# A two-layer hybrid DiT kernel: x turned for the router in pieces, picks from two parts, and a reordered seam between the layers

## The chip, the cores and the metric

The kernel runs on one core of one Trainium2 chip. The metric is the time of one execution on the device in microseconds (us); lower is better.

## What is computed

512 latent tokens and 256 context tokens of width 1024 go through two layers, in float32. A layer is an attention part (gated linear attention, neighbourhood attention, sliding window attention) and a mixture of 16 experts, in which each expert picks its tokens. Cut to what matters here:

```python
def expert_choice_ffn(h, w_router, w_gate, w_up, w_down):
    bsz, n, _ = h.shape
    cap = CAPACITY_FACTOR * n // N_EXPERTS      # 64 of 512 latent tokens, 32 of 256 context tokens
    aff = jax.nn.softmax(jnp.einsum('bnd,de->bne', h, w_router).astype(jnp.float32), axis=-1)
    g, idx = lax.top_k(aff.transpose(0, 2, 1), cap)
    xs = h[bidx, idx]
    hid = silu(xs @ w_gate) * (xs @ w_up)       # per expert
    y = (hid @ w_down) * g
    return jnp.zeros_like(h).at[bidx, idx].add(y)

for l in range(DEPTH):                          # update_ctx only in the first layer
    x = x + gt_a * rms_norm(mix @ w_out[l], g_post_a)
    xc = xc + cgt_a * rms_norm(mix_c @ w_out[l], g_post_a)         # if update_ctx
    h = modulate(rms_norm(x, g_pre_f), sh_f, sc_f)
    x = x + gt_f * rms_norm(expert_choice_ffn(h, ...), g_post_f)
    hc = modulate(rms_norm(xc, g_pre_f), csh_f, csc_f)              # if update_ctx
    xc = xc + cgt_f * rms_norm(expert_choice_ffn(hc, ...), g_post_f)
```

## The kernel before, in words

Tokens stand in tiles of 128: four latent tiles (0 to 3) and, in the first layer, two context tiles (4 and 5), which come first in `tiles(l)`. Each engine runs a program of its own, written out by hand and held together by semaphores; no scheduler orders anything. A function of one name, `route` or `post_att` say, exists once for each engine that has a part in it. PSUM has eight banks of 512 columns: `bank(n)`.

**Output projection and norm.** `w_out` makes one output tile of 128x1024 after the other in banks 0 to 3, two banks each, from the ring of weights (`ring`). `post_att` follows it tile by tile: ScalarE takes the sum of squares (`square`, line 613), VectorE forms the gated output and adds it to x (lines 1241 and 1245), ScalarE squares the new x (`norm_square`) and scales it into `XN` (`norm_scale`, line 630). ScalarE works with a lag: at step i it squares output i, then new x of tile i-1, then scales tile i-2. The scaled tiles are also stored in DRAM by GpSimd and SyncE, x as `xkeep` and XN as `xn_lat` and `xn_ctx`, from which the experts gather their rows.

**Turning.** When all tiles are scaled, `turn_x` transposes them on TensorE, 128x128 at a time, feature block by feature block (`KC` = 8), into banks 0 to 3. VectorE (`h_out`, line 1020) moves the latent part to `hT` with scale and shift, ScalarE (`h_ctx`) the context part, and TensorE may turn block k only when block k-2 has been moved.

**Router.** `route` multiplies `hT` by the router's weights (line 1834), sums the parts into logits (line 1839), and VectorE forms the softmax over experts. The affinities `AFF` are turned (line 1845) so that a row holds one expert's affinities: 16 rows of latent tokens, 512 wide, and from row 32 on 16 rows of context tokens. The picks are eight rounds of three VectorE instructions over 48x512: the eight largest values (line 1350), their places (1351), and their replacement by -1 (1352). Indices and values are then spread over 128 columns (`IDXW`, `VALW`), turned once more on TensorE, and give `rows_l` and `rows_c`, the row numbers of the gathers (lines 1363 and 1367). In the first layer TensorE meanwhile makes modulation rows of the next layer (`mod_rows`, line 1504, and `mod_cols`, line 1512); its program has them ahead of the turning of the picks.

**Experts.** They come in pairs. For each pair GpSimd gathers latent rows (line 545) and, in the first layer, context rows (547); TensorE turns them (line 1867) and multiplies by gate, up and down weights (1930, 2012). Weights come in units through eight slots in turn, loaded by SyncE (`big`, `work` and `ring` parts; lines 430 to 447); a slot is loaded anew when TensorE has used it. In the first layer outputs are added into DRAM by scatter-adds on GpSimd (lines 561 and 563).

**The seam.** After the last pair of the first layer GpSimd copies the context's x back into `X_CTX` (line 585), waits for that and for the scatter-adds, and reads the sums (line 595) into XN. VectorE adds the last expert's context part that TensorE has just made (line 1263). For latent tiles `whole` on TensorE adds the read sum, by a product with the identity (line 2089), and the last expert's part (line 2094) in PSUM. `output_square`, `new_x`, `next_square` and `normal` norm this, form the next layer's x and its norm; `turn_next` turns x by a product with a diagonal matrix `NORM` (line 2102), which also scales it, and `h_next` moves it to `hT`. Then the next projection starts (line 1580).

## Time and profile before

| | us |
|---|---|
| median of 3 runs | 2111.82 |
| lowest, highest | 2109.3, 2114.98 |
| profiled execution | 2108.1 |
| its span, first to last instruction | 2106.3 |

Over the span TensorE is busy for 91%, its weight loads for 43%, VectorE for 26%, ScalarE for 22% and GpSimd for 7%; the mean granted TensorE clock is 0.971 of full speed. Such shares are averages over stages with different limits. The table of 40 slices shows this: TensorE stands at 9 tenths in more than half of them, the DMA engines at 9 from a third of the span to past its middle and again over the last fifth. The rows further down are therefore read by stretch.

### The profile page before, as it was taken

What the parts mean: (1) busy time and instruction counts of PE and PEld (TensorE: products, weight loads), DVE (VectorE), ACT (ScalarE), POOL (GpSimd) and SP (SyncE); (2) the same over time, 40 slices, a digit from 0 to 9 for tenths busy, and PEclk for the clock granted to TensorE, in tenths of its full rate; (3) what the DMA queues carried; (4) which work ended last, traced back from release to release, by engine and by line L of the source; (5) the groups of instructions that cost most, each with busy time, mean ns of one, the idle gap of its engine ahead of it and who ended that gap; (6) DMA issues with size and microseconds to landing.
All of it is one profiled execution on the core that took longest, in us unless ns stands there. A gap on an engine that the chain in (4) does not pass through costs nothing.

```text
span 2106.3 us, 25003 instructions
## 1 busy us (share of the span) xinstructions
PE 1916.1 (91%) x10556; PEld 895.5 (43%) x10556; DVE 546.3 (26%) x1173; ACT 464.6 (22%) x967; POOL 157.6 (7%) x225
## 2 busy tenths in 40 slices
PE   5998998999879999999999899889993999988886
PEld 2655555774433333333333455447741333332232
DVE  1020564662240000000000402456625011111113
ACT  4132123442311011111111403124422111111111
POOL 0000010100000111101011000011001000000000
PEclk9999999999979999999999999999996999999998
DMA  9212068002469999999999512130018999999996
GB/s 404 103 40 80 3 267 348 24 12 80 180 254 418 401 403 387 388 394 400 388 385 363 202 40 80 40 138 27 8 60 324 390 427 427 425 428 427 425 428 272
DMA packets 54280, 541.80 MB, mean 257 GB/s; under 512 B 6528, under 2 KB 8704, under 8 KB 23216
## 3 DMA queue, kind: packets, MB, share of 16 engines
q1 hardware_dynamic: 36704, 488.82, 56.5%
q0 software_dynamic: 17344, 51.72, 7.4%
q8 instruction: 65, 1.06, 0.2%
q14 instruction: 23, 0.19, 0.0%
q10 hardware_dynamic: 144, 0.01, 0.0%
HBM read 516.80 MB, written 23.72 MB: 257 GB/s over the span
## 4 chain that ended last, share of the span: by engine, by line
PE 75%; DMA 13%; DVE 6%; ACT 3%; issue 2%; SPq 0%; POOL 0%; DVEq 0%; POOLq 0%; ACTq 0%
PE ps L1930 15%; PE ps L1580 10%; PE ps L2012 8%; PE ps L1804 7%; PE ps L1558 5%; PE ps L1938 5%; DMA ring<-in_wstream 5%; DMA work<-in_wstream 3%; DMA big<-in_wstream 3%; PE ps L1752 3%; PE ps L2019 2%; PE ps L1884 2%; PE ps L1690 2%; PE ps L1504 2%; PE ps L1550 1%
## 5 line engine op out<-in xcount | busy, mean ns | idle before, releaser
L1930 PE MATMUL ps<-ring,work 128*64 128x512 f32 x1536 | 347.2, 605 | 16.1 <-DMA ring<-in_wstream 11.7
L1423 DVE TENSOR_TENSOR work<-glao,ps 128x512 f32<-128x512 f32 x31 | 21.3, 687 | 795.3 <-ACT glao L882 411.6
L1930 PEld LDWEIGHTS ps<-ring,work 128*64 128x64 f32 x1536 | 110.0, 139 | 246.7 <-issue 230.5
L1580 PE MATMUL ps<-hT,ring 128*128 128x512 f32 (+1 forms) x592 | 206.3, 507 | 3.3 <-issue 2.6
L2012 PE MATMUL ps<-big,work 128*64 128x512 f32 x704 | 164.6, 605 | 2.1 <-ACT work L842 2.1
L1580 PEld LDWEIGHTS ps<-hT,ring 128*128 128x128 f32 x592 | 112.1, 190 | 96.1 <-issue 86.4
L1804 PE MATMUL ps<-ring,hT 128*128 128x512 f32 x320 | 138.7, 592 | 0.0
L1938 PE MATMUL ps<-ring,work 128*32 128x512 f32 x1024 | 119.6, 597 | 0.0
L1558 PE MATMUL ps<-ring,hT 128*128 128x384 f32 (+3 forms) x384 | 110.9, 451 | 0.0
L710 ACT ACTIVATE work<-ps,work 128x512 f32<-128x512 f32 (+2 forms) x120 | 81.9, 684 | 77.2 <-DVE work L1163 44.7
L1930 PE MATMUL ps<-big,work 128*64 128x512 f32 x384 | 86.5, 595 | 13.5 <-DMA big<-in_wstream 13.5
L1804 PEld LDWEIGHTS ps<-ring,hT 128*128 128x128 f32 x320 | 60.6, 191 | 73.6 <-issue 73.6
L1159 DVE TENSOR_REDUCE work<-ps 128x2 f32<-128x1024 f32 (+2 forms) x60 | 73.3, 1221 | 61.2 <-PE ps L1701 58.4
L1558 PEld LDWEIGHTS ps<-ring,hT 128*128 128x128 f32 x384 | 70.7, 190 | 39.6 <-issue 15.3
L2012 PEld LDWEIGHTS ps<-big,work 128*64 128x64 f32 x704 | 46.1, 138 | 92.7 <-issue 88.9
L1504 PE MATMUL ps<-ring,silu_c 128*32 128x512 f32 x384 | 52.9, 678 | 26.5 <-DMA ring<-in_wstream 24.7
L1752 PE MATMUL ps<-work,big 128*64 128x128 f32 x960 | 65.7, 279 | 5.4 <-DVE hT L1202 5.4
L646 ACT ACTIVATE big<-ps 128x512 f32<-128x512 f32 (+1 forms) x41 | 20.8, 508 | 205.4 <-PE ps L1580 201.8
L891 ACT ACTIVATE glao<-ps 128x512 f32<-128x512 f32 x16 | 9.6, 597 | 239.6 <-PE ps L1930 239.6
L1938 PEld LDWEIGHTS ps<-ring,work 128*32 128x32 f32 x1024 | 28.5, 109 | 77.0 <-issue 77.0
L882 ACT ACTIVATE glao<-ps 128x512 f32<-128x512 f32 x15 | 9.0, 597 | 234.7 <-PE ps L1930 234.7
L1752 PEld LDWEIGHTS ps<-work,big 128*64 128x64 f32 x960 | 51.2, 137 | 18.9 <-DVE hT L1202 8.8
(311 smaller groups left out, 2219.2 us busy)
## 6 DMA issues: line engine op xcount, KB each, us to landing
ring<-in_wstream SPq DMA_DIRECT2D x150, 2048.0 KB, 13.0
big<-in_wstream SPq DMA_DIRECT2D x68, 2048.0 KB, 15.3
hT<-in_wstream SPq DMA_DIRECT2D x12, 1024.0 KB, 31.1
work<-in_wstream SPq DMA_DIRECT2D x12, 1024.0 KB, 33.8
x_kept<-big POOLq DMA_DIRECT2D x14, 512.0 KB, 8.5
big<-x_kept POOLq DMA_DIRECT2D x12, 512.0 KB, 6.0
xn_lat<-big POOLq DMA_DIRECT2D x8, 512.0 KB, 11.1
big<-in_x_all SPq DMA_DIRECT2D x6, 512.0 KB, 7.5
```

What stands on the lines that cost most here:

```text
L710: S.activation(PR[2 * (q % 2) + j][:, 0:nl + CTX], head_scores(q, nl)[:, j, :], ACT.Exp, bias=st["neg"][:, j:j + 1], scale=SCALE, accum_ou ...
L1159: link(V.reduce_max(st["max"], head_scores(p, nl), AX))
L1504: last = T.matmul(ob[32 * j:32 * j + 32, :], CS32[:, kc, :], u[:, kc, :], start=kc < 4, stop=kc >= 4)
L1558: last = T.matmul(bank(n % 4, k_), hTv[:, kc, t * P:(t + 1) * P], v[:, kc, 0:k_], start=kc == 0, stop=kc == KC - 1)
L1580: last = T.matmul(bank(n % 4, tn), uw[:, j * D + kc * P:j * D + kc * P + P], hTv[:, kc, t0:t0 + tn], start=kc == 0, stop=kc == KC - 1)
L1690: T.matmul(place[j], q[j], k[j][:, k0:k0 + nl], start=False, stop=True)
L1752: T.matmul(PV[HD * i:HD * i + HD, :], TM[:, keys[i][j], c:c + HD], PTP[q % 2][:, i, j * P:(j + 1) * P], start=j == 0, stop=j == n - 1)
L1804: return T.matmul(bank(2 * (i % 2) + j), hTv[:, kc, t * P:(t + 1) * P], u[:, kc, :], start=kc == 0, stop=kc == KC - 1)
L1884: last = T.matmul(ob, PT_L[half][:, t * P:(t + 1) * P], YL[half], start=True, stop=True)
L1930: last = T.matmul(bank(m)[64 * h:64 * h + 64, :], XST[:, kc, e, 0:CAP_L], gate_up[j][kk][:, m * D + h * 512:m * D + (h + 1) * 512], start= ...
L1938: last = T.matmul(bank(2)[32 * g:32 * g + 32, :], XST[:, kc, e, CAP_L:CW], gate_up[j][kk][:, g * 512:(g + 1) * 512], start=kc == 0, stop=k ...
L2012: last = T.matmul(bank(6 if ctx_too else 3)[64 * g:64 * g + 64, :], HT[:, kc, 0:CAP_L], down[j][kc % 4 // 2][:, kc % 2, h * 512:(h + 1) * ...
```

## The change

- **x is turned in pieces.** In the first layer, TensorE turns the two context tiles after output 2 of `w_out` (16 transposes into banks 4 to 7). `turn_lat` replaces `turn_x`: it turns latent tiles 0 to 2, block by block, before it waits for the norm of the last tile, and then the last tile alone. ScalarE and VectorE share the moves to `hT` (`ACT_K`, `DVE_K`); `h_out` and the "f" part of `h_ctx` are gone. ScalarE squares and scales each tile in its own step, without the lag.
- **Picks from two parts.** The 512 latent tokens stand in two parts of 256, in rows 0 to 15 and 32 to 47 of the turned affinities; the context in rows 64 to 79. Eight rounds go over 80x256, the last without replacement. 64 picks of each part result, one list in falling order, the other reversed; for each place the greater of the two values is kept (`LATER`), and with it its index, plus 256 for the second part. Values are turned ahead of indices.
- **The seam.** The sum of the second latent tile is added by VectorE instead of by an identity product (`SUMMED`). Half of the context's `h_next` moves from ScalarE to VectorE. The orders of `new_x`, `normal` and `next_square` differ, and `outputs` of the last expert precedes the context's first `next_square` on ScalarE.
- **Copies.** GpSimd issues the two copies of the context's x in pair 4 of the experts, not after the last pair.

The diff, cut to its core:

```diff
+        SUMMED = [NLT, NLT + 1, 1]
...
                         if i < PAIRS - 1:
                             scatter_add(2 * i + 1)
-                    for c in range(NCT):
-                        pool.dma_start(X_CTX[:, c, :], xkeep[LAT + c * P:LAT + (c + 1) * P, :]).then_inc(sem(f"x_rows{NLT + c}"), 16)
+                        if i == PAIRS // 2:
+                            for c in range(NCT):
+                                pool.dma_start(X_CTX[:, c, :], xkeep[LAT + c * P:LAT + (c + 1) * P, :]).then_inc(sem(f"x_rows{NLT + c}"), 16)
...
-                for i in range(len(ts) + 2):
...
+                for i, t in enumerate(ts):
+                    act.wait_ge(sem("wo"), i + 1 + l * PER["wo"])
+                    square(ps[:, (i % 2) * D:(i % 2) * D + D], SQUARES, ss[:, t:t + 1], "psq")
+                    if i == 2 and l < DEPTH - 1:
+                        for k in range(KC // 2):
+                            act.wait_ge(sem("xT"), k // 2 + 1 + before("xT", l, "f"))
+                            last = h_part(k, 1, hTv[:, k, LAT:TOK], bank(4 + k // 2, CTX, k % 2 * CTX))
+                        last.then_inc(sem("h_ctx"), 1)
+                    if i == n - 1:
+                        for k in ACT_K:
+                            act.wait_ge(sem("xT"), turned + k + 1)
+                            h_part(k, 0, hTv[:, k, 0:3 * P], bank(4 + k % 4, 3 * P)).then_inc(sem("h_ctx"), 1)
+                    norm_square(l, "f", i, t)
+                    norm_scale(l, "f", i, t)
+                for k in range(KC // 2):
+                    act.wait_ge(sem("xT"), turned + KC + 1 + 2 * (k // 2))
+                    last = h_part(k, 0, hTv[:, k, 3 * P:LAT], bank(k // 2, P, k % 2 * P))
+                last.then_inc(sem("h_ctx"), 1)
...
-                h_next(range(KC // 2), 0)
+                h_next(range(KC // 2, KC), 0).then_inc(sem("h_ctx"), 1)
                 next_square(l, 0)
-                h_next(range(KC // 2, KC), 0).then_inc(sem("h_ctx"), 1)
...
+                next_square(l, 3)
                 act.wait_ge(sem("xT"), 2 + before("xT", l + 1, "a"))
                 h_next(range(KC // 2, KC), 1).then_inc(sem("h_ctx"), 1)
-                next_square(l, 3)
                 act.wait_ge(sem("xT"), 4 + before("xT", l + 1, "a"))
...
                     output_square(l, NLT + 1)
...
+                    outputs(i, e)
                     next_square(l, NLT)
-                    outputs(i, e)
                     next_square(l, NLT + 1)
...
+                def h_lat(ks):
+                    for k in ks:
+                        dve.wait_ge(sem("xT"), turned + k + 1)
+                        h_part(k, 0, hTv[:, k, 0:3 * P], bank(4 + k % 4, 3 * P)).then_inc(sem("h_t"), 1)
...
-                for i, t in enumerate(tiles(l)):
+                for i, t in enumerate(ts):
+                    if i == n - 1:
+                        h_lat(DVE_K[0:1])
...
-                    if i:
-                        rms(l, "f", i - 1, tiles(l)[i - 1])
-                rms(l, "f", i, t)
+                    if i == 2 and l < DEPTH - 1:
+                        for k in range(KC // 2, KC):
+                            dve.wait_ge(sem("xT"), k // 2 + 1 + before("xT", l, "f"))
+                            last = h_part(k, 1, hTv[:, k, LAT:TOK], bank(4 + k // 2, CTX, k % 2 * CTX))
+                        last.then_inc(sem("h_t"), 1)
+                    if i == n - 1:
+                        h_lat(DVE_K[1:3])
+                    rms(l, "f", i, t)
+                h_lat(DVE_K[3:])
+                for k in range(KC // 2, KC):
+                    dve.wait_ge(sem("xT"), turned + KC + 2 + 2 * (k % 4 // 2))
+                    last = h_part(k, 0, hTv[:, k, 3 * P:LAT], bank(k // 2, P, k % 2 * P))
+                last.then_inc(sem("h_t"), 1)
...
-                for i in range(NCT, NT):
-                    new_x(i)
-                    if i > NCT:
-                        normal(i - 1)
+                dve.wait_ge(sem("x_rows1"), ACC_READ)
+                dve.wait_ge(sem("comb"), 3)
+                V.tensor_tensor(XN[:, 1, :], XN[:, 1, :], ps[:, D:2 * D], ALU.add).then_inc(sem("acc"), 1)
+                new_x(2)
+                new_x(3)
+                dve.wait_ge(sem("xT"), 1 + before("xT", l + 1, "a"))
+                h_next(range(KC // 2), 0)
+                new_x(4)
+                normal(2)
+                normal(3)
+                new_x(5)
+                normal(4)
+                normal(5)
                 dve.wait_ge(sem("xT"), 2 + before("xT", l + 1, "a"))
                 h_next(range(KC // 2), 1)
-                normal(NT - 1)
...
                 for r in range(CAP_L // 8):
...
-                    link(V.match_replace(dst, VALS[0:48, sl], src, -1.0))
...
+                    link(V.max(VALS[0:m, sl], src))
+                    found = V.max_index(idxu[0:m, sl], VALS[0:m, sl], src)
+                    link(V.match_replace(dst, VALS[0:m, sl], src, -1.0) if r + 1 < CAP_L // 8 else found)
+                wide = [(0, 2, slice(0, CAP_L)), (32, 2, slice(None, None, -1))] + ([(64, 4, slice(0, CAP_C))] if ctx_too else [])
+                for src, dst, done in ((VALS, VALW, "vals"), (idxu, IDXW, "picked")):
+                    for r0, n, order in wide:
+                        last = V.tensor_copy(v3(dst[r0:r0 + NE, :], n), src[r0:r0 + NE, order].unsqueeze(1).broadcast_to([NE, n, P // n]))
+                    last.then_inc(sem(done), 1)
+                idx_t, val_t = bank(5, m), bank(4, m)
                 dve.wait_ge(sem("pickedT"), 1 + l * PER["pickedT"])
...
+                link(V.tensor_copy(APART, val_t[:, 32:32 + NE]))
+                V.tensor_tensor(LATER, APART, val_t[:, 0:NE], ALU.is_gt)
+                V.tensor_tensor(VALT[:, 0:NE], APART, val_t[:, 0:NE], ALU.max)
+                dve.wait_ge(sem("pickedT"), 2 + l * PER["pickedT"])
+                link(V.tensor_copy(IDXT[:, 0:NE], idx_t[:, 0:NE]))
+                link(V.scalar_tensor_tensor(APART, idx_t[:, 32:32 + NE], float(2 * P), IDXT[:, 0:NE], ALU.add, ALU.subtract))
+                link(V.tensor_tensor(APART, APART, LATER, ALU.mult))
+                link(V.tensor_tensor(IDXT[:, 0:NE], IDXT[:, 0:NE], APART, ALU.add))
...
+                    last = V.tensor_copy(rows_l[r, :], IDXT[r, 0:NE].rearrange("p (a e) -> p e a", e=2)[:, half, :])
...
+                    if i == 2 and ctx_too:
...
+                        pe.wait_ge(sem("xn"), NCT + before("xn", l, "f"))
+                        for k in range(KC):
+                            for t in range(NCT):
+                                last = T.transpose(bank(4 + k // 2, P, (NCT * (k % 2) + t) * P), XN[:, NLT + t, k * P:(k + 1) * P], ident)
+                            if k % 2:
+                                last.then_inc(sem("xT"), 1)
...
+            def turn_lat(l):
...
+                pe.wait_ge(sem("xn"), n - 1 + before("xn", l, "f"))
...
+                for k in range(KC):
+                    if k >= 4:
+                        by, ks = ("h_ctx", ACT_K) if k - 4 in ACT_K else ("h_t", DVE_K)
+                        pe.wait_ge(sem(by), done + ks.index(k - 4) + 1 + before(by, l, "f"))
+                    for t in range(3):
+                        last = T.transpose(bank(4 + k % 4, P, t * P), XN[:, t, k * P:(k + 1) * P], ident)
+                    last.then_inc(sem("xT"), 1)
+                pe.wait_ge(sem("xn"), n + before("xn", l, "f"))
+                for b in (0, 2, 1, 3):
+                    for k in (2 * b, 2 * b + 1):
+                        last = T.transpose(bank(b, P, k % 2 * P), XN[:, 3, k * P:(k + 1) * P], ident)
+                    last.then_inc(sem("xT"), 1)
+                pe.wait_ge(sem("h_t"), done + 5 + before("h_t", l, "f"))
+                pe.wait_ge(sem("h_ctx"), done + 5 + before("h_ctx", l, "f"))
...
+                pe.wait_ge(sem("vals"), 1 + l * PER["vals"])
+                T.transpose(bank(4, m), VALW[0:m, :], ident[0:m, 0:m]).then_inc(sem("pickedT"), 1)
                 pe.wait_ge(sem("picked"), 1 + l * PER["picked"])
                 T.transpose(bank(5, m), IDXW[0:m, :], ident[0:m, 0:m]).then_inc(sem("pickedT"), 1)
-                pe.wait_ge(sem("vals"), 1 + l * PER["vals"])
-                T.transpose(bank(4, m), VALW[0:m, :], ident[0:m, 0:m]).then_inc(sem("pickedT"), 1)
...
-                    pe.wait_ge(sem(f"x_rows{t}"), ACC_READ)
+                    summed = t in SUMMED
...
                         pe.wait_ge(sem("acc"), NCT)
-                    elif t >= 2:
-                        pe.wait_ge(sem("y_used"), t - 1 + before("y_used", l, "f"))
...
-                        T.matmul(bank(2 * (t % 2) + h), ident, XN[:, t, h * 512:(h + 1) * 512], start=True, stop=False)
+                    elif t == 2:
+                        pe.wait_ge(sem("y_used"), 1 + before("y_used", l, "f"))
+                    elif t == 3:
+                        pe.wait_ge(sem("acc"), NCT + 1)
+                    if not summed:
+                        pe.wait_ge(sem(f"x_rows{t}"), ACC_READ)
...
+                            T.matmul(bank(2 * (t % 2) + h), ident, XN[:, t, h * 512:(h + 1) * 512], start=True, stop=False)
...
-                        last = T.matmul(bank(2 * (t % 2) + h), PT_L[0][r, t * P:(t + 1) * P], YL[1][r, :], start=False, stop=True)
+                        last = T.matmul(bank(2 * (t % 2) + h), PT_L[0][r, t * P:(t + 1) * P], YL[1][r, :], start=summed, stop=True)
```

The order on TensorE from the end of the first layer's output projection to the turning of the affinities, before (line 1804 is the projection, 1528 the transposes of x, 1834 the router, 1504 a modulation row, 1845 the affinities):

```order
397 L1804 MATMUL ps<-ring,hT 128x512 x80
398 L1528 MATMUL ps<-cst,big 128x128 x48
399 L1834 MATMUL ps<-hT,router 32x512 x8
400 L1834 MATMUL ps<-hT,router 32x256 x8
401 L1839 MATMUL ps<-cst,work 128x16 x6
402 L1504 MATMUL ps<-ring,silu_c 32x512 x8
403 L1845 MATMUL ps<-cst,work 48x128 x4
404 L1798 MATMUL ps<-work,ones 128x512 x4
```

And now, with 1867 the projection, 1896, 1916 and 1921 transposes of x, 1930 the router and 1942 the affinities:

```order
397 L1867 MATMUL ps<-ring,hT 128x512 x32
398 L1896 MATMUL ps<-cst,big 128x128 x16
399 L1867 MATMUL ps<-ring,hT 128x512 x48
400 L1916 MATMUL ps<-cst,big 128x128 x24
401 L1921 MATMUL ps<-cst,big 128x128 x8
402 L1930 MATMUL ps<-hT,router 32x512 x8
403 L1930 MATMUL ps<-hT,router 32x256 x8
404 L1935 MATMUL ps<-cst,work 128x16 x6
405 L1567 MATMUL ps<-ring,silu_c 32x512 x8
406 L1942 MATMUL ps<-cst,work 80x128 x2
```

The 48 transposes that stood in one block behind the projection stand in three places: 16 inside it, 24 and 8 behind it; four transposes of affinities are two.

VectorE's order from the end of the last round of picks in the first layer to the row numbers, before:

```order
435 L1351 MAX_INDEX idxu<-work 48x8
436 L1352 MATCH_REPLACE work<-work 48x512
437 L1354 CAST work<-idxu 16x128
438 L1355 CAST work<-idxu 16x128
439 L1357 COPY work<-work 16x128
440 L1358 COPY work<-work 16x128
441 L1363 CAST rows_l<-ps 64x8 x2
442 L1367 CAST rows_c<-ps 32x8 x2
```

And now; the lines from 1417 to 1424 are the merge of the two parts:

```order
440 L1407 MAX_INDEX idxu<-work 80x8
441 L1413 COPY work<-work 16x128 x3
442 L1413 CAST work<-idxu 16x128 x3
443 L1417 COPY work<-ps 128x16
444 L1418 TENSOR_TENSOR work<-work,ps 128x16
445 L1419 TENSOR_TENSOR work<-work,ps 128x16
446 L1421 COPY work<-ps 128x16
447 L1422 SCALAR_TENSOR_TENSOR work<-ps,work 128x16
448 L1423 TENSOR_TENSOR work<-work 128x16
449 L1424 TENSOR_TENSOR work<-work 128x16
450 L1427 CAST rows_l<-work 64x8 x2
451 L1431 CAST rows_c<-ps 32x8 x2
```

The last round has no replacement. Between the turned picks and `rows_l` stand seven more instructions of 128x16, and the copies of the values precede the casts of the indices.

GpSimd's order in the last pairs of the first layer's experts, before (561 and 563 are scatter-adds, 545 and 547 gathers, 585 the copies of the context's x, 595 the reads of the sums):

```order
89 L561 DMA acc_lat<-work,add_l 1024x512
90 L563 DMA acc_ctx<-work,add_c 1024x256
91 L561 DMA acc_lat<-work,add_l 1024x512
92 L563 DMA acc_ctx<-work,add_c 1024x256
93 L585 DMA hT<-x_kept 128x1024 x2
94 L595 DMA big<-acc_ctx 128x1024 x2
95 L595 DMA big<-acc_lat 128x1024 x4
```

And now, from the middle pair on, where 566 and 568 are scatter-adds, 550 and 552 gathers and 591 the copies:

```order
77 L550 DMA big<-xn_lat,rows_l 128x1024
78 L552 DMA big<-xn_ctx,rows_c 64x1024
79 L566 DMA acc_lat<-work,add_l 1024x512
80 L568 DMA acc_ctx<-work,add_c 1024x256
81 L591 DMA hT<-x_kept 128x1024 x2
82 L566 DMA acc_lat<-work,add_l 1024x512
83 L568 DMA acc_ctx<-work,add_c 1024x256
84 L550 DMA big<-xn_lat,rows_l 128x1024
85 L552 DMA big<-xn_ctx,rows_c 64x1024
```

Five pairs of scatter-adds follow the copies, and the reads of the sums then follow the last of these (not shown).

## Rows read from the trace of the kernel before

**Rows 1.** Busy time by stretch: us, PE, PEld, DVE, ACT, POOL, clock, DMA share, GB/s.

```profile
640.00:700.00 60.00, 60.00 (x432) 20.84 (x424) 4.18 (x11) 8.36 (x18) 8.27 (x6) 1.00 1.02 404
...
1625.00:1634.00 9.00, 6.87 (x21) 2.76 (x22) 0.00 (x0) 4.18 (x9) 0.97 (x1) 0.50 0.20 58
1650.00:1660.00 10.00, 10.00 (x46) 3.28 (x44) 0.00 (x0) 1.18 (x2) 0.00 (x0) 0.92 1.01 431
```

**Rows 2.** TensorE in order of time, first layer: start, us, engine, line, what.

```profile
574.13 2.79 PE L1834 MATMUL ps<-hT,router 128*32 128x512 f32 x32 [0.75 <-DVE hT L1020]
...
579.34 3.31 PE L1504 MATMUL ps<-ring,silu_c 128*32 128x512 f32 x16
582.58 0.88 PE L1845 MATMUL ps<-cst,work 128*48 128x128 f32 x4
...
597.50 1.05 PE L1512 MATMUL ps<-cst,glao 128*128 128x2 f32 x8 [0.72 <-ACT glao L697]
...
609.94 1.94 PE L1867 MATMUL ps<-cst,big 128*128 128x128 f32 x8 [7.10 <-issue]
```

**Rows 3.** ScalarE at the end of the output projection, first layer, then second.

```profile
557.69 1.02 ACT L613 ACTIVATE work<-ps 128x1024 f32<-128x1024 f32 x1 [10.07 <-PE ps L1804]
...
563.13 2.17 ACT L630 ACTIVATE big<-big,small 128x1024 f32<-128x1024 f32 x2
...
1578.74 1.02 ACT L613 ACTIVATE work<-ps 128x1024 f32<-128x1024 f32 x1 [10.07 <-PE ps L1804]
```

**Rows 4.** TensorE between the layers, in order of time.

```profile
1146.70 0.66 PE L1906 MATMUL ps<-cst,work 128*128 128x128 f32 x4
...
1155.27 1.15 PE L1894 MATMUL ps<-work 32*128 32x256 f32 x16 [0.16 <-ACT work L855]
...
1194.27 10.56 PE L1580 MATMUL ps<-hT,ring 128*128 128x512 f32 x32 [2.07 <-issue]
```

**Rows 5.** VectorE, first layer: last new x, first and after last pick, row numbers.

```profile
560.59 1.22 DVE L1245 TENSOR_TENSOR big<-big,work 128x1024 f32<-128x1024 f32 x1
...
584.21 0.69 DVE L1350 MAX8 work<-work 48x8 f32<-48x512 f32 x1
...
601.51 0.22 DVE L1354 CAST work<-idxu 16x128 f32<-16x128 uint32 x1
...
602.81 0.33 DVE L1367 CAST rows_c<-ps 32x8 uint32<-32x8 f32 x2
```

**Rows 6.** TensorE, second layer: router, first expert.

```profile
1594.33 1.93 PE L1834 MATMUL ps<-hT,router 128*32 128x512 f32 x16 [0.91 <-DVE hT L1020]
...
1628.62 16.83 PE L1930 MATMUL ps<-ring,work 128*64 128x512 f32 x64 [2.13 <-ACT work L834]
```

**Rows 7.** GpSimd's queue between the layers.

```profile
1132.87 1.80 POOL L585 DMA_DIRECT2D hT<-x_kept  x2
1154.56 1.05 POOL L595 DMA_DIRECT2D big<-acc_ctx  x2 [19.89 <-DMA hT<-x_kept]
```

**Rows 8.** Landing times of L563, the scatter-add of context rows.

```profile
DMA to landing us min/median/max: 15.0/15.7/16.3
```

**Rows 9.** VectorE between the layers: the context rows' sums.

```profile
1159.37 2.35 DVE L1263 TENSOR_TENSOR big<-big,ps 128x1024 f32<-128x1024 f32 x2 [7.07 <-DMA big<-acc_ctx]
```

**Rows 10.** ScalarE between the layers: half of the context's turned tiles.

```profile
1174.80 1.93 ACT L757 ACTIVATE hT<-ps,cols 128x256 f32<-128x256 f32 x4 [2.41 <-PE ps L2102]
```

**Rows 11.** GpSimd's queue, second layer: the first gather.

```profile
1620.10 1.01 POOL L545 DMA_INDIRECT big<-xn_lat,rows_l  x1 [17.88 <-DVE rows_l L1363]
```

**Rows 12.** SyncE's queue, second layer: weight loads.

```profile
1598.44 0.99 SPq L430 DMA_DIRECT2D big<-in_wstream  x2
...
1601.63 0.45 SPq L447 DMA_DIRECT2D work<-in_wstream  x1
1635.19 10.63 SPq L444 DMA_DIRECT2D ring<-in_wstream  x4
```

**Rows 13.** Landing times of L545, the gather of token rows: min, median, max.

```profile
DMA to landing us min/median/max: 4.2/11.0/12.9
```

100 lines of the change are left out of this document (52 added, 48 removed).

## The prediction, made before the changed kernel had run

> **What bounds the kernel now.** I read the busy times by stretch first [rows 1]. From 640 to 700 us, in the first layer's experts, TensorE is busy for 60.00 of 60 us. From 1650 to 1660 us, in the second layer's, it is the DMA engines that have no gap: share 1.01 at 431 GB/s. Whatever lies ahead of the first layer's experts therefore moves the end one for one through TensorE. What lies ahead of the second layer's moves it one for one if the weight stream itself moves. It can: between 1625 and 1634 us the DMA share is 0.20 [rows 1], because all eight slots are full and the next load waits until the first expert has emptied one.
>
> So the kernel has three places where a chain over several engines, not a stream, sets the time. They are the router of each layer (557.69 to 609.94 us, and its like from 1578.74 to 1628.62) and the seam between the layers (about 1150 to 1194.27 us). The chain of waits runs there through ScalarE, VectorE, GpSimd and short TensorE pieces. The change touches just these.
>
> **A. The first layer's router.** TensorE comes to the router's product at 574.13 us [rows 2], 16.4 us after ScalarE began on the last tile's output at 557.69 [rows 3].
>
> 1. Two context tiles are now turned inside the output projection: 16 transposes. Nothing hides them, TensorE runs without a gap there. Four such transposes took 0.66 us [rows 4], so 16 cost at most 2.6; I take 2.5. Their inputs are ready by some 7 us: the norms of those tiles belong to the two outputs before, and before each output ScalarE has waited some 10.07 us for TensorE [rows 3]. The evacuations are shared by two engines that are idle most of each tile, so they cost nothing.
> 2. Three latent tiles are turned while the last one is normalised. New x of the last tile is there 4.1 us after 557.69, as before (560.59 + 1.22) [rows 5]. Its norm was the second of two scaling passes of ScalarE that took 2.17 us together and ended at 565.30, 7.6 us after [rows 3]; the other one is now done earlier, so I put it at 6.9 us. ScalarE's four and VectorE's three passes over 384 columns lie in the 4.1 us, and in ScalarE's square, while each waits for the other. Then come 8 transposes, 1.3 us by the price above or 1.94 us as at 609.94, where the clock was low [rows 2], and a tail of two short passes, some 0.6 us: 8.8 to 9.5 us; with release times between engines 9.8. The router starts 16.4 - 9.8 = 6.6 us sooner, less the 2.5: 4.1 us.
> 3. From the router to the turning of the affinities are 8.45 us (574.13 to 582.58) [rows 2]. The same 16 products of 128x512 take 3.31 us at 579.34, and 1.93 us at 1594.33 [rows 2, 6]: the first is the low clock of 1.2 GHz, the second 2.4 GHz. TensorE now works in short bursts between 560 and 570 us, where it had one 8 us run of transposes ahead of the router. So the router may meet the low clock, and the products behind it the high one. Bounds: 1.3 us won (products at 2.4 GHz), 3.3 lost (router and logits at 1.2). I take 1.0 lost, since one of the two low stretches replaces the other. Two transposes in place of four give 0.3. The affinities are turned 3.4 us sooner.
> 4. The picks: VectorE's eight rounds run from 584.21 to 601.51, 2.16 us each [rows 5]. Each is three passes over 512 elements of 0.69 us; a pass of 1024 takes 1.22, so 256 elements are worth 0.53 - 0.27 = about 0.27 us, and a pass over 256 takes 0.42. Eight rounds of 1.36 us less the last replacement are 10.4 us instead of 17.3: 6.9 us won. The bound below is no gain, if search passes do not follow the width.
> 5. But TensorE has something to do meanwhile: modulation rows up to 598.55 (597.50 + 1.05) [rows 2], 16 us of them from the affinities on, and the picks are turned behind them. With 3.4 us won they end at 595.15. The picks are ready at 582.58 - 3.4 + 0.5 + 0.4 + 10.4 + 0.7 = 591.2. What was the picks is now **the modulation rows**, and 4 us of the picks' gain have no use in this layer. Behind it the two parts are merged: a release of 0.35 us, seven steps of 0.2 to 0.25 on VectorE, four casts of 0.17: 2.5 us to the row numbers, at 597.7. They were there at 603.14 (602.81 + 0.33) [rows 5]. **A = 5.5 us won**, between 2 and 8. The gather, its turning at 609.94 and the first expert follow at the same distance, on a quiet DMA as before. SyncE's loads into the ring are freed by the same modulation rows and move with them.
>
> **B. The seam.** GpSimd issues the two copies of the context's x at 1132.87 and waits for them until 1154.56 [rows 7]. The last scatter-add was issued just ahead of the copies and lands in 16.3 us at most [rows 8], near 1148.5. With the copies moved to the middle of the experts GpSimd is free there, 5.7 us sooner. But the sums at 1159.37 [rows 9] also need the product that ends at 1155.27 + 1.15 = 1156.42 [rows 4]. They start then: 2.9 us won, not 5.7. Behind them one tile's sum moves from TensorE to VectorE (1.22 us there, one identity pass less on TensorE), and one of the two lots of ScalarE's four context passes, 1.93 us [rows 10], moves to VectorE, which has a gap there. ScalarE was the engine that the last tiles' new x waited for. Following tile by tile I come to 1189.3 for the next projection, which stood at 1194.27 [rows 4]. **B = 5.0 us won**: 2.9 from the start, 2.1 from the order; between 2 (the order gives nothing and the start less) and 6.5.
>
> The moved copies cost 1 MB of DMA in experts where TensorE never waits for a load; they and SyncE's loads share the engines. GpSimd does not wait for them. The next scatter-add comes some 34 us later (16 experts lie between 609.94 and 1146.70 [rows 2, 4]), the copies needed 20 us in their old place. I cost them at nothing.
>
> **C. The second layer's router.** There are no context tiles, so step 1 is absent, and no modulation rows, so the picks' gain counts in full. Router: 1594.33 [rows 6] is 15.6 us after ScalarE began on the last output at 1578.74 [rows 3]; with 9.8 it is 5.8 sooner. Clock: 1.0 lost. Fewer transposes and a shorter copy: 0.5 won. Picks: 6.9 won. Merge: 1.8 lost against the two casts there were. The gather is issued 10.4 us sooner: at about 1610 in place of 1620.10 [rows 11].
>
> Now it meets the weights. The eighth slot's load is issued at 1601.63 [rows 12] and lands near 1621, ahead of the old gather's data. The scaling passes now follow their own tile, so the stores of two tiles leave a tile earlier, in a quiet stretch: 4 stores of 0.5 MB, 2.1 MB at 0.43 MB/us are 5 us of DMA out of the way. The last of them holds SyncE's loads back until 1598.44 [rows 12]. The weights should be in by 1616. A gather took 4.2 us on a quiet DMA and 11.0 as the median [rows 13]; for one that runs 5.5 us beside weights I take 8. The first expert then starts 6.5 us sooner than at 1628.62 [rows 6]. The load at 1635.19 [rows 12] and the stream behind it follow. **C = 6.5 us won**, between 3.4 and 9.
>
> The Trainium skill (DMA: Bandwidth & Descriptors, Anatomy of one DMA — SWDGE (gpsimd) path) gives 2.0 us plus bytes over 436e3 for such a transfer, 3.2 us as an estimate for this gather. The landing row [rows 13] disagrees, 11.0 us as the median; by the page's figure C would be about 10.
>
> **Sum.** 5.5 + 5.0 + 6.5 = 17.0 us. The profiled execution has a span of 2106.3 us and a time of 2108.1; it would be 2091.1. The median of the three runs shown is 2111.8, 3.7 us higher; I put the sum against it: **2094.8 us**.
>
> **The rivals.**
>
> - *The clock.* Router, logits and the products behind them all at 1.2 GHz in both layers, since TensorE's bursts are too thin. Against it: the clock was back within the 8 us before the router in both layers. A 3.2, C 5.0, B 5.0: 2098.6 us. The Trainium skill (TensorE: Matmul & The Clock Gate, Part 1: The HAM clock gate) has it that the low clock is the default state and only activity lifts it; by that rule spreading the transposes works against this change.
> - *The early gather waits for the weights* in full, 11.0 us: C 3.4, 2097.9 us.
> - *The picks do not get shorter with their width.* A 2.1 (the rows are ready at about 601), B 5.0, C 3.8: 2100.9 us.
> - *The seam gives 2 only*, since another engine takes over as its bound: 2097.8 us.
> - *More than forecast*: the clock stays high and the gather finds the DMA free. A 8, B 5, C 9: 2089.8 us.
> - *It does not do what it says*: the turned tiles are evacuated late, by engines that sit in other waits, and the early turning is lost. A 0, B 5, C 2: 2104.8 us.
> - *Slower*: the moved copies block GpSimd's queue in the experts. The software queue takes transfers in order, so a scatter-add behind them lands late, the next outputs wait for it, and TensorE stops. It decides once the copies take over 34 us, the distance to the next scatter-add; to outweigh the 17 us and the 0.3% they would have to hold it for some 57 us. In their old place they took 20. At 60 us: about 2120 us.
>
> **Chances.** Forecast 0.47; clock 0.14; gather 0.12; seam 0.10; picks 0.06; more 0.06; slower 0.03; does not do what it says 0.02. The likeliest is the forecast. The steps' own ends, 2, 2 and 3.4 us, are unlikely to meet; 2086 to 2105 us holds more than 8 in 10 with the runs' own spread of 3 us to each side. A measurement tells about 0.3%, 6.3 us, from no change. Faster by more than that: 0.93; within: 0.04; slower: 0.03.
>
> **What would show it.** In the trace after: transposes of 128x128 inside the first layer's projection, 2.5 us of them; the router 4 us earlier in the first layer and near 6 in the second, with its duration (2.79 and 1.93 before) telling the clock; rounds of picks of 1.36 us; in the first layer VectorE waiting for TensorE behind the picks; GpSimd's reads of the sums near 1148.5 less A; the second layer's first gather landing in 6 to 11 us. I am wrong if the search passes stay near 0.68 us, if the modulation rows no longer end behind the picks, or if the second layer's DMA idle time grows by what its router wins.

## The result, and the profile after

The changed kernel takes 2094.42 us (median of 7 runs, 2089.93 to 2100.13) against 2111.94 us for the kernel before (7 runs, 2108.06 to 2114.98): 17.5 us less, ratio 0.9917, 95% interval 0.9904 to 0.9931. The forecast was 2094.8 us, 17.0 us less than the runs shown then.

The profiled execution took 2099.6 us, one of the two slowest of the seven, so its absolute times can't be laid beside those of before. Its last output of the first layer's projection comes 7.5 us later than before. Only 1.9 us of that belong to the change. The other 5.7 us stand ahead of the first thing that the change touches, and over all traces of this study ScalarE's start on the last output lies between 557.7 and 569.3 us. I therefore compare distances within a stage.

The page's head, first the kernel before, then after (span, and busy time of each engine with its share):

```profile
span 2106.3 us, 25003 instructions
PE 1916.1 (91%) x10556; PEld 895.5 (43%) x10556; DVE 546.3 (26%) x1173; ACT 464.6 (22%) x967; POOL 157.6 (7%) x225
```

```profile
span 2097.3 us, 25019 instructions
PE 1926.6 (92%) x10548; PEld 901.6 (43%) x10548; DVE 535.1 (26%) x1196; ACT 470.0 (22%) x975; POOL 158.0 (8%) x225
```

TensorE is busy for 10 us more although it has less to do; busy time grows when a product runs at the low clock, and the shares don't show where. TensorE's timeline in the first layer, after (start, duration, line, what):

```profile
522.03 1.91 PE L1896 MATMUL ps<-cst,big 128*128 128x128 f32 x16
...
565.63 3.28 PE L1916 MATMUL ps<-cst,big 128*128 128x128 f32 x24 [0.48 <-issue]
572.36 1.97 PE L1921 MATMUL ps<-cst,big 128*128 128x128 f32 x8 [3.46 <-ACT big L636]
575.15 4.49 PE L1930 MATMUL ps<-hT,router 128*32 128x512 f32 x32 [0.82 <-DVE hT L1259]
580.64 1.51 PE L1935 MATMUL ps<-cst,work 128*128 128x16 f32 x12 [1.00 <-ACT work L836]
582.08 3.57 PE L1567 MATMUL ps<-ring,silu_c 128*32 128x512 f32 x16
585.58 0.42 PE L1942 MATMUL ps<-cst,work 128*80 128x128 f32 x2
...
600.04 1.05 PE L1575 MATMUL ps<-cst,glao 128*128 128x2 f32 x8 [0.71 <-ACT glao L703]
600.95 0.27 PE L1952 MATMUL ps<-cst,work 80*128 80x80 f32 x1
...
615.13 5.84 PE L2026 MATMUL ps<-ring,work 128*64 128x512 f32 x16 [2.32 <-issue]
```

ScalarE begins on the last output at 565.18. The router comes 9.97 us later (before 16.44, [rows 2, 3]), the first expert 49.95 us later (before 57.55). The router itself is longer than before, 4.49 for 2.79 us, and the products at 582.08 are still slow. The picks' transposes at 600.95 follow the last modulation column without a wait: they are queued behind it. VectorE's timeline shows the same from its side; a pass over 80x256 takes 0.42 us, and after the last spread it waits 2.79 us for the transposes:

```profile
586.49 0.42 DVE L1406 MAX8 work<-work 80x8 f32<-80x256 f32 x1
...
587.03 0.42 DVE L1407 FIND_INDEX8 idxu<-work 80x8 uint32<-80x256 f32 x1
...
597.78 0.68 DVE L1413 CAST work<-idxu 16x128 f32<-16x128 uint32 x3
601.26 0.17 DVE L1417 COPY work<-ps 128x16 f32<-128x16 f32 x1 [2.79 <-PE ps L1952]
...
602.83 0.32 DVE L1431 CAST rows_c<-ps 32x8 uint32<-32x8 f32 x2
```

The second layer, after, on TensorE, and below it GpSimd's first gather and SyncE's next load:

```profile
1585.80 3.47 PE L1930 MATMUL ps<-hT,router 128*32 128x512 f32 x16 [0.82 <-DVE hT L1259]
...
1619.09 15.92 PE L2026 MATMUL ps<-ring,work 128*64 128x512 f32 x64 [2.13 <-ACT work L854]
```

```profile
1607.75 1.01 POOL L550 DMA_INDIRECT big<-xn_lat,rows_l  x1 [12.51 <-DVE rows_l L1427]
```

```profile
1624.76 10.63 SPq L449 DMA_DIRECT2D ring<-in_wstream  x4
```

From ScalarE's start on the last output (1575.90) to the first expert are 43.19 us, before 49.88 [rows 3, 6].

All stages in one table, in us, worked out from such rows. "Last output" is ScalarE's start on it, "seam product" the end of the product for the last expert's context rows, "end" the end of TensorE's last product, some 14.1 us ahead of the end of the span:

| distance | before | after | after, again |
|---|---|---|---|
| last output to router, layer 1 | 16.44 | 9.97 | 9.97 |
| router to affinities | 8.45 | 10.43 | 10.52 |
| affinities to last modulation column | 15.97 | 15.51 | 15.51 |
| from there to the row numbers | 4.59 | 2.06 | 2.07 |
| last output to first expert | 57.55 | 49.95 | 49.94 |
| first expert to seam product | 541.18 | 540.69 | 540.77 |
| seam product to next projection | 37.85 | 33.56 | 33.57 |
| projection to last output, layer 2 | 384.47 | 386.52 | 386.48 |
| last output to first expert, layer 2 | 49.88 | 43.19 | 43.40 |
| first expert to end | 463.56 | 464.13 | 464.29 |

With the 1.9 us for the context's transposes this makes 5.7 + 0.5 + 4.3 - 2.05 + 6.7 - 0.6 = 14.6 us for this execution, the low end of the interval of the medians (14.6 to 20.3 us). The term of -2.05 us is mostly a stretch of low clock that only some traces have (below).

### The profile page after: what moved, and what is told of

The parts are those of the page before. It is cut to its first block, busy times and chain, and to the rows that moved or that the text cites. A ratio compares the mean times of both kernels' runs of the same rounds, so it can differ in the third digit from the quotient of the medians.

```text
span 2097.3 us, 25019 instructions
## 1 busy us (share of the span) xinstructions
PE 1926.6 (92%) x10548; PEld 901.6 (43%) x10548; DVE 535.1 (26%) x1196; ACT 470.0 (22%) x975; POOL 158.0 (8%) x225
## 4 chain that ended last, share of the span: by engine, by line
PE 80%; DMA 11%; DVE 5%; ACT 2%; issue 2%; SPq 0%; DVEq 0%; ACTq 0%; POOLq 0%
PE ps L2026 16%; PE ps L1643 10%; PE ps L2108 9%; PE ps L1867 7%; PE ps L2034 5%; PE ps L1621 5%; DMA ring<-in_wstream 5%; DMA work<-in_wstream 3%; DMA big<-in_wstream 3%; PE ps L1815 3%; PE ps L2115 3%; PE ps L1567 2%; PE ps L1980 2%; PE ps L1753 2%; PE ps L1613 1%
```

## The experiments

Each median stands beside one of the kernel before, taken together with it, and the ratio is against that one; the changed kernel itself was run again only beside 9 and 10. The stages come from one profiled execution of each kernel. Code is cut to the edit, and `...` marks what is left out.

**1. The copies alone.** In the kernel before:

```diff
-                    for c in range(NCT):
-                        pool.dma_start(X_CTX[:, c, :], ...)
+                        if i == PAIRS // 2:
+                            for c in range(NCT):
+                                pool.dma_start(X_CTX[:, c, :], ...)
```

> The kernel before with one edit: the two copies of the context's x go out in pair 4 of the first layer's experts, as in the change. Theory (a wait at the start of the seam shifts all of it): the context's sums start at the end of the product for the last expert (0.15 us after it, not 2.95), everything behind moves by 2.8 us, the next projection starts 35.0 us after that product instead of 37.85; about 2109.1 us. Rival (TensorE's own work, which ends 7 us after that product, sets the seam): under 1 us won, 2111 us. Rival (copies load GpSimd's queue in the experts): TensorE shows waits in the experts and their 541.2 us grow.

2110.74 us against 2112.6, ratio 0.9985 (0.9974 to 0.9996). The sums start 0.15 us after the seam product, as expected, but the projection comes 36.23 us after it: 1.6 us won, not 2.8. TensorE's timeline, first one row of before, then of this kernel:

```profile
1166.89 1.13 PE L2094 MATMUL ps<-work 64*128 64x512 f32 x4 [1.54 <-ACT work L860]
```

```profile
1156.84 7.09 PE L2013 MATMUL ps<-big,work 128*64 128x512 f32 x32
1163.85 1.98 PE L2090 MATMUL ps<-big,cst 128*128 128x512 f32 x4
1165.77 1.13 PE L2095 MATMUL ps<-work 64*128 64x512 f32 x4
1166.83 1.98 PE L2090 MATMUL ps<-big,cst 128*128 128x512 f32 x4
```

Before, TensorE waited 1.54 us for ScalarE between the identity product and the last expert's part. Now it has no wait there, and up to the second block of turning its own work follows without a gap: that is the new bound, and 1.6 us is the wait that went. The experts take 541.28 us, as before: the copies cost nothing there.

**2. The order alone.** The changed kernel, copies behind the last pair again (the diff above, reversed).

> The changed kernel with the copies put back behind the last pair: the seam's new order without its earlier start. Theory: the sums start 2.95 us after the last product again; the order alone gives 1.5 us against the kernel before (36.4 us from the product to the projection), so 2.8 us over the changed kernel, about 2097.2 us. Rival (the order needs no early start, or the reverse, the early start is only of use with the order): seam as fast as in the changed kernel (33.6 us), 2094.4 us, or as slow as before (37.9 us), 2098.7 us.

2096.95 us, ratio 0.9926 (0.9907 to 0.9945), 2.5 us over the changed kernel by the medians, and the seam takes 34.74 us although the sums start 3.84 us after the product. The order alone thus gives 3.1 us, where I had 1.5. TensorE now waits where before it had work, 1.55 us ahead of the first turning:

```profile
1162.03 3.84 PE L2201 MATMUL ps<-hT 128*128 128x128 f32 x32 [1.55 <-DVE hT L1327]
...
1174.91 7.38 PE L2201 MATMUL ps<-big 128*128 128x128 f32 x64 [2.85 <-DVE big L1327]
1184.37 10.56 PE L1642 MATMUL ps<-hT,ring 128*128 128x512 f32 x32 [2.07 <-DVE hT L1298]
```

The 64 products of the second block take 7.38 us here. In the changed kernel the same 64 take 9.01 us, without a wait between them in either. The clock differs: in the first 5 us of the block the granted clock is 0.66 of full speed there and 1.00 here. The changed kernel's row, then its busy times from the start of the block, then this kernel's (columns as in [rows 1], the clock is the third from the end):

```profile
1178.31 9.01 PE L2202 MATMUL ps<-big 128*128 128x128 f32 x64 [2.12 <-DVE big L1328]
```

```profile
1178.31:1183.31 5.00, 5.00 (x30) 5.00 (x31) 3.63 (x8) 2.19 (x6) 0.81 (x2) 0.66 0.98 368
```

```profile
1174.91:1179.91 5.00, 5.00 (x45) 5.00 (x46) 3.79 (x9) 2.87 (x8) 0.82 (x2) 1.00 0.99 420
```

So the 4.3 us that both give together hide a loss of 1.6 us to the clock. With this block at 7.38 us the changed kernel's seam would take 31.9 us, an estimate that experiments 6, 9 and 10 bear out with 31.88. At an equal clock the order gives 3.1 us and the early start another 2.8 on top of it. That is more than the 1.6 it gives under the old order, where TensorE's own work took over as the bound.

**3. The picks alone**, in the kernel before. The edit is the part of the diff on `AFF`, `VALS`, `idxu` and the merge, with

```diff
+                a = [AFT0[0:m, 0:2 * P], AFT1[0:m, 0:2 * P]]
```

> The kernel before with the picks from two parts alone. Theory: in the first layer the modulation rows end last, the row numbers come 2.0 us behind them, 2.5 us won of the 6.9 that the rounds lose; in the second layer the gather is issued 5.4 us earlier but its rows land behind the weights that are loaded until about 1621 us, so that the first expert starts only some 3 us earlier. 5.5 us in all, 2106.4 us. Rival (the gather takes no notice of the weights): 5.4 us won in the second layer, 7.9 in all, 2104.0 us. Rival (search passes do not follow their width): rounds of 2.16 us, nothing won.

2106.87 us, ratio 0.9975 (0.9959 to 0.9992). In the edit the search passes go over 256 columns. First layer: 54.91 us from the last output to the first expert, 2.6 won. Second layer: the gather is issued 14.96 us after the affinities, not 20.40, but the first expert gains only 1.3 us, 1.9 without a difference of 0.56 us that this trace has ahead of the router. The gather in GpSimd's queue, then the turning of its rows on TensorE, then the busy times by 2 us (PE, PEld, DVE, ACT, POOL, clock, DMA share, GB/s):

```profile
1617.97 1.01 POOL L545 DMA_INDIRECT big<-xn_lat,rows_l  x1 [12.50 <-DVE rows_l L1374]
```

```profile
1625.92 1.94 PE L1878 MATMUL ps<-cst,big 128*128 128x128 f32 x8 [9.96 <-issue]
```

```profile
1619.00:1621.00 2.00, 0.00 (x0) 0.00 (x0) 0.00 (x0) 0.00 (x0) 0.00 (x0) 0.50 1.01 422
1621.00:1623.00 2.00, 0.00 (x0) 0.00 (x0) 0.00 (x0) 0.00 (x0) 0.00 (x0) 0.50 1.02 422
1623.00:1625.00 2.00, 0.00 (x0) 0.00 (x0) 0.00 (x0) 0.00 (x0) 0.00 (x0) 0.50 0.80 324
```

The rows are turned 7.95 us after the issue, before 4.44 us. No engine works, the DMA engines are full with weights, and the gather's rows come when these are in. The rival that the gather takes no notice of them falls. The stages of this trace add up to about 3.5 us, less than the 5.7 of the medians. 0.8 us are lost in the seam, which this edit does not touch: the old copies land later after the last product there, so the sums start 3.70 us behind it instead of 2.95.

**4. The turning alone**, in the kernel before: `turn_lat`, the transposes within `w_out`, and `post_att` without the lag.

```diff
-                turn_x(l, "f")
+                turn_lat(l)
```

> The kernel before with x turned in pieces alone (with it the norm of each tile in its own step). Theory: first layer, router 6.5 us sooner after the last output, 1.9 us for the context's 16 transposes, 1.9 us lost to the low clock in router and logits: affinities and everything behind 2.6 us sooner. Second layer: router 5.7 us sooner, 1.6 us lost to the clock, weights in 4 us sooner too, so the first expert starts some 4.1 us sooner. 6.7 us in all, 2105.2 us. Rival (the picks were on the path, so the router's gain is only taken over by another wait, as with the modulation rows): first layer 0.

2104.76 us, ratio 0.9963 (0.9949 to 0.9978). Router 9.96 us after the last output, affinities 8.62 us behind it, first expert at 50.71 us: 6.8 won, 4.9 with the context's transposes taken off. I had expected 2.6 because I took the clock's 1.9 us from the changed kernel's trace. Here the first modulation row behind the router was fast (1.92 us) and only the router slow (4.20 us). Second layer: 3.5 us sooner, 4.1 expected.

That makes 8.4 us, and the total won by the medians is 7.8. Part of it is lost again in the seam, which takes 41.16 us instead of 37.85 although this edit does not touch it. The copies of the context's x are still in their old place, and land later after the last product: the sums start 4.60 us behind it, TensorE waits 3.07 us for ScalarE where it waited 1.54, and behind this wait its clock is low for a while (0.66 of full speed from 1165 to 1170 us):

```profile
1165.95 1.61 PE L2168 MATMUL ps<-work 64*128 64x512 f32 x4 [3.07 <-ACT work L878]
```

So the old seam is no fixed price: 37.85, 36.23, 38.61 and 41.16 us in the four traces that have its order, the second with the copies moved. The 4.3 us of the changed kernel are measured against the first; against the last, which has x turned in the same way, its seam wins 7.6.

**5. The picks' transposes ahead of the last modulation row**, in the changed kernel:

```diff
                     for k, n in enumerate(MOD_ROUTE):
                         mod_cols(n, SGL, bank(1))
+                        if k + 2 == len(MOD_ROUTE):
+                            pe.wait_ge(sem("grow_out"), 1 + before("grow_out", l, "f"))
+                            picks_turned()
                         if k + 1 < len(MOD_ROUTE):
...
```

> The changed kernel, with the turning of the picks ahead of the last of the four modulation rows on TensorE instead of behind all of them. Theory (in the first layer the modulation rows end last and hold the picks): the picks' transposes run as soon as VectorE has spread them, some 2.1 us sooner, and the last modulation row runs while the gather is on its way, where TensorE waits 6.7 us; first expert 2.1 us sooner, about 2092.3 us. Rival (the picks themselves end last): nothing won, 2094.4 us. Rival (the later release of the ring's weights by the modulation rows delays the experts' loads): TensorE waits for loads in the first expert, 2 us lost.

In the first layer the trace has it as the theory says: first expert 47.32 us after the last output, with the router as slow as in the changed kernel (4.49 us), so 2.6 us won, and no wait in the experts (540.30 us). TensorE's timeline:

```profile
597.39 0.26 PE L1947 MATMUL ps<-cst,work 80*128 80x80 f32 x1 [0.43 <-DVE work L1413]
598.01 0.29 PE L1949 MATMUL ps<-cst,work 80*128 80x80 f32 x1 [0.36 <-DVE work L1413]
598.23 3.33 PE L1567 MATMUL ps<-ring,silu_c 128*32 128x512 f32 x16
602.26 1.05 PE L1575 MATMUL ps<-cst,glao 128*128 128x2 f32 x8 [0.70 <-ACT glao L703]
```

The total doesn't tell it: 2094.42 us beside 2114.34 for before, ratio 0.9906 (0.9883 to 0.9929), which overlaps with the changed kernel's. In this trace the second layer gives 1.8 us back: first expert 44.98 us after the last output instead of 43.19, with the rows turned 8.67 us after the gather's issue instead of 7.27. The edit does not touch that layer. Experiments 2 and 8, which don't either, have 44.65 and 43.98 us, so this distance differs by up to 1.8 us between kernels that are the same there.

**6. TensorE kept busy**, in the changed kernel, in `turn_lat` and in the seam ahead of `turn_next(2, 4)`:

```diff
+                pe.wait_ge(sem("y_used"), n - 1 + before("y_used", l, "a"))
+                for _ in range(20):
+                    T.transpose(bank(0, P, 2 * P), ident, ident)
...
+                for _ in range(12):
+                    T.transpose(bank(7, P, 2 * P), ident, ident)
```

> The changed kernel with TensorE kept busy by transposes whose result nobody uses: 20 while the last tile is normalised (both layers) and 12 in the seam ahead of the second tile pair. Theory (TensorE's clock falls because of the 3.5 us gap ahead of the last tile): the router takes 2.8 and 1.9 us again instead of 4.2 to 5.4 and 3.5, the last 8 transposes 1.3 instead of 2.0; first layer 1.5 to 2.5 us sooner, unless the low clock then comes with the products behind, second layer 1.7 to 2.2 us; about 2091.0 us. Rival (the clock falls later anyway, as in the kernel before, where it was low behind the router): router short, but the logits or modulation rows slow, under 0.5 us won in each layer, 2094 us.

2090.13 us, ratio 0.9894 (0.9872 to 0.9916). The seam takes 31.88 us instead of 33.56 (the 64 products of `turn_next` 7.41 instead of 9.01 us). The second layer's router takes 1.92 us and its affinities come 5.43 us behind it instead of 6.99. The first layer's router stays slow:

```profile
567.11 2.35 PE L1920 MATMUL ps<-cst 128*128 128x128 f32 x20
570.73 1.09 PE L1924 MATMUL ps<-cst,big 128*128 128x128 f32 x8 [1.28 <-ACT big L636]
572.86 4.48 PE L1933 MATMUL ps<-hT,router 128*32 128x512 f32 x32 [1.03 <-DVE hT L1259]
...
1579.46 1.92 PE L1933 MATMUL ps<-hT,router 128*32 128x512 f32 x16 [1.03 <-DVE hT L1259]
```

The seam takes 31.88 us in all three traces with the idle transposes (this one, 9 and 10), and 33.6 in all five with the same seam and without them, so this is no accident of one execution. The theory holds in two of three places. In the second layer most of the gain is lost again: the earlier gather takes 9.03 us instead of 7.27.

**7. The eighth slot's load held back**, in the changed kernel:

```diff
                     for u in range(SLOTS, FFN_UNITS):
                         s, g = laps(l, u)
+                        if u == MORE - 1:
+                            sp.wait_ge(sem("xs_rows"), fetched(l, 1))
```

> The changed kernel, with the load of the eighth weight slot in the second layer held back until the rows of the first gather have landed. Theory (the gather waits for the weights that are loaded beside it): the rows land 4.3 us after the issue instead of 7.3 to 8.6, the first expert starts 3 us sooner, and the held load fits in where the DMA engines had nothing to do before the next load; 2091.4 us. Rival (the stream's total decides, so an idle gap is only moved): 2094.4 us. Rival (the eighth slot comes too late for the second expert): TensorE waits once more, slower by up to 2 us.

Gather and turning, then SyncE's queue, in which the load in two halves now goes out at 1613:

```profile
1608.94 1.01 POOL L552 DMA_INDIRECT big<-xn_lat,rows_l  x1 [12.50 <-DVE rows_l L1429]
```

```profile
1613.42 1.94 PE L1965 MATMUL ps<-cst,big 128*128 128x128 f32 x8 [6.49 <-issue]
```

```profile
1613.35 0.33 SPq L454 DMA_DIRECT2D hT<-in_wstream  x1
1613.72 0.43 SPq L454 DMA_DIRECT2D work<-in_wstream  x1
1623.32 10.63 SPq L451 DMA_DIRECT2D ring<-in_wstream  x4
```

4.48 us from issue to turning instead of 7.27, first expert at 40.88 us instead of 43.19 (43.19 to 44.98 over the five traces that have this layer as the changed kernel), although the router was slower in this execution (affinities 7.98 us behind it, not 6.99). The rest of the program stays at 464.28 us, so nothing is given back. Total 2092.33 us, ratio 0.9906 (0.9884 to 0.9928): the trace settles it, the total alone would not.

**8. The moved copies three times over**, in the changed kernel:

```diff
+                                for rep in range(2):
+                                    at = (2 * c + rep) * P
+                                    pool.dma_start(out[at:at + P, :], xkeep[...]).then_inc(...)
```

> The changed kernel with four more copies of 0.5 MB, from the stored x to the output tensor (rows that the end of the kernel overwrites), beside the two moved ones in pair 4: the moved work three times over. Theory (there is room for the copies): TensorE shows no wait in the experts, whose 540.7 us stay within 1 us; 2094.4 us. Rival (software-queue transfers run in order, and a scatter-add behind the copies lands late): two copies took 20 to 26 us beside the weights, six take some 60 to 75, which is over the 34 us to the next scatter-add; the outputs' buffers are reused late and TensorE waits, up to 30 us, 2125 us.

2093.69 us, ratio 0.9918 (0.9894 to 0.9941). The first expert to the seam product takes 540.57 us. Landing times of the two moved copies in the changed kernel, then of the four added ones here, then busy times of the stretch here:

```profile
DMA to landing us min/median/max: 20.3/23.1/25.9
```

```profile
DMA to landing us min/median/max: 22.1/27.7/33.1
```

```profile
955.00:990.00 35.00, 35.00 (x248) 11.84 (x248) 1.38 (x2) 3.33 (x6) 7.54 (x9) 1.00 1.02 417
```

Each of the six lands within 33 us of its issue, where I had put 60 to 75 for all: they run side by side, and TensorE has no gap. The next scatter-add is issued some 28 us after the last copy, not 34, so it may meet the end of the copies; the experts' 540.57 us show no cost of it. The prediction's slower rival has no ground here.

**9 and 10. All three edits together, and more idle transposes.** The first is experiments 5, 6 and 7 in one; the second has 26 for 20 and six more behind the router's product:

```diff
-                for _ in range(20):
+                for _ in range(26):
...
                 last.then_inc(sem("router_parts"), 1)
+                for _ in range(6):
+                    T.transpose(bank(0, P, 2 * P), ident, ident)
```

> The changed kernel with all three edits that each moved something alone: the picks turned ahead of the last modulation row, TensorE kept busy in the two gaps, the eighth slot's load held until the first gather has landed. Theory (three separate waits, so the gains add up): 2.6 us in the first layer, 1.7 in the seam and up to 1.8 behind it, 1.5 for the second layer's router and 3 for its gather, 9 to 10 us in all, about 2085 us. Rival (a router that comes earlier only finds the gather waiting longer for the weights, or the held load then lands late): 5 us, 2089.5 us.

> As the one with all three edits, with 26 idle transposes in the gap instead of 20 and 6 more behind the router. Theory (what is left of the gap still lets the clock fall in the first layer): the first layer's router 2.8 us and its first modulation row 1.9 us, 1.5 to 2 us won there; about 2083.5 us. Rival (the clock falls there for another reason, the pause between the last transposes and the router, which no idle work can fill): router 4.5 us as before, nothing won or a few tenths lost, 2085.3 us.

The first: **2082.91 us** (5 runs, 2081.34 to 2088.89), ratio 0.9860 (0.9839 to 0.9881), the best of all kernels here, 11.8 us below the changed kernel beside it (2094.73, experiment 11). The second: 2084.93 us, ratio 0.9863 (0.9842 to 0.9885), which can't be told from the first. In us: last output to first expert 44.33 and 43.20, seam 31.88 in both, second layer 39.92 and 39.98. The first layer's router takes 2.79 us in both, so the six transposes more were not what it needed; with 20 it was slow in experiment 6 and fast here. The first modulation row behind it takes 2.77 and 1.92 us, and the first expert comes 1.1 us sooner in the second; its second projection takes 386.23 us instead of 384.72 and gives that back. The first one's TensorE:

```profile
570.96 2.79 PE L1935 MATMUL ps<-hT,router 128*32 128x512 f32 x32 [1.03 <-DVE hT L1261]
...
576.17 2.77 PE L1569 MATMUL ps<-ring,silu_c 128*32 128x512 f32 x16
```

The gains add up but for the second layer's gather, which still takes 6.26 us instead of 4.48: it is issued earlier, and the weights ahead of the held load are not in yet (the DMA engines carry them for another 5 us, in experiment 7 for 1).

**11. The changed kernel again**, beside these two.

> The changed kernel itself once more, beside the two others on the same chip. 2094.4 us; the trace tells how much its stages differ from one execution to the next: the first layer's router path (49.95 us from the last output to the first expert) within 1 us, the start of the program within some 10 us, the second projection with or without a stretch of low clock (386.5 or 384.7 us).

2094.73 us, ratio 0.9922 (0.9901 to 0.9944). Its stages are in the table above and repeat those of the changed kernel to about 0.2 us.

## Why the prediction was right, step by step

The medians give 17.5 us for 17.0 forecast, and that is closer than the mechanism was: the rows of the profiled execution add up to 14.6 us. The clock cost more than the sum had for it. Ahead of the affinities of the two layers it took 2.0 and 1.6 us net in this trace, where the sum had 0.7 and 0.5; in the seam and at the projection behind it 1.6 and 1.7, where the sum had nothing. The seam's new order gave more than forecast, and in part these errors cancelled. What else the medians hold beyond the 14.6 us no trace shows.

- **Turning, first layer.** The 16 context transposes took 1.91 us (2.5 taken). The router came 9.97 us after the last output (9.8). Right.
- **The clock.** I took 1.0 us lost, since one low stretch would replace the other. Both were low, the router (4.49 us) and the first modulation row (3.57, before 3.31): 2.0 us lost net of the two transposes fewer, where the sum had 0.7, and 2.6 instead of 3.4 us won up to the affinities. The term was mis-sized, and it isn't a constant: router to affinities took 8.45 us before, 9.8 to 10.5 in the changed kernel and experiments 2 and 5 to 8, 8.62 with the turning alone, 7.91 and 7.26 in experiments 9 and 10. By the Trainium skill (TensorE: Matmul & The Clock Gate, Part 1: The HAM clock gate) activity lifts the clock, and experiment 6 agrees in two of three places: 1.92 for 3.47 us, 7.41 for 9.01 us. In the third, the first layer's router, it does not: 4.48 for 4.49 us.
- **Picks.** A pass of 256 took 0.42 us as worked out, eight rounds less the last replacement 10.5 us (10.4). The prediction's working for the pass ("0.53 - 0.27") is muddled, but its 0.27 us for 256 elements follows from the two durations it names. That the modulation rows end last in the first layer was right. What it costs was put at 4 us and is 2.6: the last spread ends 12.88 us after the affinities (12.0 by the forecast's times), the modulation columns after 15.51 (16.0), and experiment 5 gives 2.6 us back. The merge took 2.06 us to the row numbers (2.5). First layer in all 5.7 us (5.5).
- **Seam.** 4.3 us for 5.0. The total hides two errors. The order was put at 2.1 us and gives 3.1 (experiment 2), with an identity product of 1.98 us taken from TensorE among its parts; no run tells the parts apart. And the sum has a clock term for both routers but none for the seam, where the second block of turning meets a low clock and loses 1.6 us. The 2.9 us for the start come out as 2.8 at an equal clock, but only together with the new order. Under the old one they are 1.6 (experiment 1), against that experiment's expectation that everything behind moves with the sums: I had followed ScalarE and VectorE tile by tile, but not TensorE, which had one wait of 1.54 us and otherwise no slack until its second block.
- **A loss that I had not listed.** In four of the nine traces with the new seam (the changed kernel twice, experiments 8 and 10) the granted clock is at the low level at the start of the projection too; its first 44.72 us of work then take 46.43, and the stage up to the last output 386.2 to 386.5 us in place of 384.6 to 384.8. None of the four traces with the old order has it, and experiment 1 lost as much elsewhere in that stage. Whether the change causes it stays open; it costs 1.7 us where it occurs.
- **Second layer.** Router 9.90 us after the last output (9.8), clock 1.6 lost net of the shorter turning (0.5 taken), gather issued 9.5 us sooner (10.4), landed after 7.3 us (8), first expert 6.7 us sooner (6.5). Right, but by luck in part: two errors of about 1 us cancel, the clock and the gather's landing. Experiment 3 confirms the reason for the gather's time, experiment 7 the remedy.
- **Copies in the experts** cost nothing, with room for three times as much.

## What to carry to other kernels

When a chain over several engines is shortened, ask at each join which other chain arrives next; here, with the picks alone, the modulation rows and the merge left 2.6 us of the 6.9 by which the rounds are shorter, and the weights 1.3 to 1.9 us of the 5.4 by which the gather came sooner. Moving one transposition, or holding one load that nobody needed yet, gave part of it back. A transfer that others wait for should not be issued behind bulk loads that have slack. Where total times scatter by several us, distances between two rows in one stage decide more than the total can: two traces of the changed kernel agree to about 0.2 us. But look at every stage, not only at the one that was edited. In kernels that are the same there, the old seam took 37.85 to 41.16 us and the second layer up to its first expert 43.19 to 44.98. Compare parts at an equal granted clock before calling them not additive.
